# Gate rows of a two-block decoder kernel computed in the norms' gaps instead of inside the feed-forward loops

## What is computed

```
mod = cond @ ada_w[l] + ada_b[l]
sh1, sc1, g1, sh2, sc2, g2, sh3, sc3, g3 = split(mod, 9)
hn = rms_norm(h, norm_g[l, 0]) * (1 + sc1) + sh1
h = h + 0.5 * g1 * swiglu(hn, ffn1_w_in[l], ffn1_w_out[l])
hn = rms_norm(h, norm_g[l, 1]) * (1 + sc2) + sh2
h = h + g2 * (mixed(hn @ w_in[l]) @ w_out[l])
hn = rms_norm(h, norm_g[l, 2]) * (1 + sc3) + sh3
h = h + 0.5 * g3 * swiglu(hn, ffn2_w_in[l], ffn2_w_out[l])
```

## Time and profile before

| | us |
|---|---|
| median of 3 runs | 2203.54 |
| lowest, highest | 2200.04, 2205.11 |
| the profiled execution | 2208.43 |
| its span | 2206.4 |
| PE busy in the span | 2117.9 |
| DVE busy | 1413.1 |
| ACT busy | 1109.4 |
| POOL busy | 60.6 |

### The profile page before, as it was taken

The page is one execution under the profiler, slowest core; times in us unless marked ns, Lnnn a source line. Parts: engine busy times, 40 slices in busy tenths (PEclk is TensorE's granted clock), DMA queues, the critical chain, the costliest instruction groups (busy, mean ns, idle before and its releaser), DMA issues.

```text
span 2206.4 us, 33404 instructions
## 1 busy us (share of the span) xinstructions
PE 2117.9 (96%) x13908; PEld 1910.1 (87%) x13908; DVE 1413.1 (64%) x1866; ACT 1109.4 (50%) x1757; POOL 60.6 (3%) x40
## 2 busy tenths in 40 slices
PE   8999899999999999999999999899999999989999
PEld 7798788998979888999899898589989998868998
DVE  5466568786455748878655665665576556566555
ACT  5347535445426835444555553555555555355554
POOL 0110000000020000000001000000000100000000
PEclk9999999999999999999899998899999999889999
DMA  7353278895544238988455432145545554213553
GB/s 265 115 191 115 77 276 332 345 365 187 172 137 150 96 114 320 367 336 332 168 184 179 155 134 93 63 154 188 182 152 199 173 188 149 81 58 134 181 184 133
DMA packets 56165, 409.54 MB, mean 186 GB/s; under 512 B 6608, under 2 KB 6992, under 8 KB 7888
## 3 DMA queue, kind: packets, MB, share of 16 engines
q1 hardware_dynamic: 46512, 330.20, 42.1%
q10 hardware_dynamic: 9504, 77.21, 8.8%
HBM read 406.34 MB, written 1.05 MB: 185 GB/s over the span
## 4 chain that ended last, share of the span: by engine, by line
PE 85%; DVE 7%; ACT 5%; issue 2%; DMA 1%; POOL 0%; DVEq 0%; ACTq 0%; SPq 0%; POOLq 0%
PE bank L555 24%; PE bank L556 24%; PE bank L557 24%; PE bank L974 3%; PE bank L1049 1%; DVE weights_low L388 1%; PE bank L1699 1%; PE bank L907 1%; ACT weights_high L377 1%; PE bank L919 1%; ACT work L435 1%; ACT scratch L452 1%; DVE work L513 1%; ACT work L436 0%; ACT weights_high L378 0%
## 5 line engine op out<-in xcount | busy, mean ns | idle before, releaser
L388 DVE TENSOR_TENSOR weights_low<-raw_weights,weights_high 128x1024 fp32r<-128x1024 f32 x584 | 699.8, 1239 | 457.2 <-ACT weights_high L377 455.6
L555 PE MATMUL bank<-h_high,weights_high 128*128 128x256 f32 x2944 | 859.3, 292 | 18.7 <-DVE h_low L524 13.1
L556 PE MATMUL bank<-h_low,weights_high 128*128 128x256 f32 x2944 | 846.9, 288 | 0.0
L557 PE MATMUL bank<-h_high,weights_low 128*128 128x256 f32 x2944 | 846.5, 288 | 0.0
L377 ACT ACTIVATE weights_high<-raw_weights 128x1024 fp32r<-128x1024 f32 x292 | 309.0, 1058 | 725.2 <-PE bank L557 681.4
L555 PEld LDWEIGHTS bank<-h_high,weights_high 128*128 128x128 f32 x2944 | 578.9, 197 | 33.9 <-DVE work L513 11.6
L556 PEld LDWEIGHTS bank<-h_low,weights_high 128*128 128x128 f32 x2944 | 579.2, 197 | 3.9 <-issue 1.9
L557 PEld LDWEIGHTS bank<-h_high,weights_low 128*128 128x128 f32 x2944 | 578.5, 197 | 0.0
L378 ACT ACTIVATE weights_high<-raw_weights 128x1024 fp32r<-128x1024 f32 x292 | 305.1, 1045 | 0.0
L555 PE MATMUL bank<-weights_high,hidden_high 128*128 128x512 f32 x608 | 237.9, 391 | 2.4 <-DVE weights_low L388 2.4
L556 PE MATMUL bank<-weights_low,hidden_high 128*128 128x512 f32 x608 | 237.6, 391 | 0.0
(11 more groups left out here) (275 smaller groups left out, 2010.7 us busy)
## 6 DMA issues: line engine op xcount, KB each, us to landing
raw_weights<-in_stream SPq DMA_DIRECT2D x310, 1024.0 KB, 4.9
work<-in_ada ACTq DMA_DIRECT2D x64, 1152.0 KB, 10.1
consts<-in_consts SPq DMA_DIRECT2D x1, 2048.0 KB, 12.5
work<-in_row ACTq DMA_DIRECT2D x2, 836.0 KB, 5.5
x<-in_x SPq DMA_DIRECT2D x1, 1024.0 KB, 4.9
out_x<-x SPq DMA_DIRECT2D x4, 256.0 KB, 2.0
gain_row<-in_final SPq DMA_DIRECT2D x1, 512.0 KB, 13.1
vec<-in_vec SPq DMA_DIRECT2D x1, 169.0 KB, 12.5
```

Source lines behind the costliest of these rows:

```text
L388: dve.tensor_tensor(low[:, c], raw[:, c], high[:, c].bitcast(F32), ALU.subtract).then_inc(m.raw_done[plan.index[name] % RAW], 1)
L555: pe.matmul(out, aH, bH, start=start, stop=False, skip_group_check=True)
L556: pe.matmul(out, aH, bL, start=False, stop=False, skip_group_check=True)
L557: return pe.matmul(out, aL, bH, start=False, stop=stop, skip_group_check=True)
```

## The change

The two products, their wait and ACT's two copies move from the loops of the feed-forward parts into the norm's gap: gate 0 ahead of the transposes of n1, gate 1 ahead of those of n2, gate 2 ahead of those of n3. They now use banks 4 and 5 (6 and 7 for the very first), whose sums DVE has read by then, which is what the wait on x_ready says. The groups row0 to row2 leave GROUPS2, so six groups a layer fewer are handed round on banks 0 to 3. ACT copies behind its last 1/rms and ahead of its first rounding of h. POOL makes the diagonals earlier: gate 0 in the feed-forward part of the stage before (behind up4 of the first block, or behind fg2_4), gate 1 still in feed-forward 1, gate 2 when mc0 has been used. The squares go to `h_temp` in `work`, so that `scratch` can hold diagonals across a norm. Behind the 16 transposes PE makes two products of the identity with itself, 128 columns, whose result is not read (`pe_keep`).

```diff
@@ ffn of pe_layer2
+            if j == 1:
+                pe.wait_ge(m["row_copied"], m.at("row_copied", 2 if n == 1 else 6))
...
-            if j in ROWS_AT[n]:
-                r = ROWS_AT[n][j][0]
-                pe.wait_ge(m["diag_ready"], m.at("diag_ready", r + 1))
-                for half in range(2):
-                    name = f"row{r}_{half}"
-                    pe_begin(pe, m, plan, name)
-                    done(name, pe.matmul(m.bank(plan, name)[:, :], m.const("ones"), diag(m, r)[:, half * 512:half * 512 + 512],
-                                         start=True, stop=True))
@@ new functions
+def row_bank(m, plan, r, half):
+    return m.ps[4 + half if r > 0 or plan.l > 0 else 6 + half]
+def pe_row(pe, m, plan, r, s):
+    pe.wait_ge(m["diag_ready"], 3 * plan.l + r + 1)
+    for half in range(2):
+        if r < 2:
+            pe.wait_ge(m.x_ready, m.at("x_ready", 4 * s + half + (1 if r > 0 or plan.l > 0 else 3)))
+        pe.matmul(row_bank(m, plan, r, half)[:, :], m.const("ones"), diag(m, r)[:, half * 512:half * 512 + 512], start=True,
+                  stop=True).then_inc(m["row_full"], 1)
+def pe_keep(pe, m, bank, n):
+    for _ in range(n):
+        pe.matmul(bank[:, 0:P], m.const("ident"), m.const("ident"), start=True, stop=True)
+def act_row(act, m, plan, r):
+    for half in range(2):
+        act.wait_ge(m["row_full"], m.at("row_full", 2 * r + half + 1))
+        act.activation(gate_row(m, r)[:, half * 512:half * 512 + 512], row_bank(m, plan, r, half)[:, :],
+                       ACT.Copy).then_inc(m["row_copied"], 1)
@@ pe_layer2
+    pe_row(pe, m, plan, 0, -1)
     pe_norm(pe, m, plan, -1, "n1")
+    pe_keep(pe, m, m.ps[6] if l > 0 else m.ps[5], 2)
     ffn(1, 0, "n1")
+    pe_row(pe, m, plan, 1, 0)
     pe_norm(pe, m, plan, 0, "n2")
+    pe_keep(pe, m, m.ps[6], 2)
...
+    pe_row(pe, m, plan, 2, 1)
     pe_norm(pe, m, plan, 1, "n3")
+    pe_keep(pe, m, m.ps[6], 2)
@@ act_layer2
     for i in range(4):
         norm_square(act, m, step, 0, PIECES_DOWN, i)
+    act_row(act, m, plan, 1)
     norm(1, "n2")
@@ norm_square
-    step(act.activation(sq_tiles(m)[:, c], m.x[:, c], ACT.Square, accum_out=stat(m, tt, 0 if first else 1)))
+    step(act.activation(h_temp(m)[:, c], m.x[:, c], ACT.Square, accum_out=stat(m, tt, 0 if first else 1)))
@@ pool_layer2
+        elif name == "mo0":
+            m.wait_consumed(pool, plan, "mc0")
+            diagonal(pool, m, l, 2)
+        elif name == "fg2_4" and plan.next is not None:
             m.wait_full(pool, plan, name)
-            diagonal(2, 32)
+            diagonal(pool, m, l + 1, 0)
```

More of the change, by code:

```diff
@@ L97, in ffn_groups @@
         out += [(f"fg{n}_{j}", "V"), (f"fu{n}_{j}", "V")]
-        if j in ROWS_AT[n]:
-            out += [(f"row{ROWS_AT[n][j][0]}_{h}", "A") for h in range(2)]
     return out
@@ L188 @@
     2: {"a_copied": 8, "conv_diag": 3, "conv_exp": 2, "conv_log": 1, "conv_normed": 2, "conv_rstd": 1, "conv_sq": 1,
[L189 to L194, removed]
+         "conv_step": 34, "down_used": 22, "fgate_exp": 22, "fgate_log": 22, "fox_l": 1, "fox_lf": 1, "gelu_act": 4,
+         "gelu_vec": 6, "gv_ready": 2, "hH_ready": 24, "h_ready": 12, "lam_exp": 1, "lam_sum": 1, "ln_rstd": 1, "ln_stat": 1,
+         "mix_high": 4, "mix_low": 4, "o_ready": 6, "o_sq": 2, "p_ready": 8, "pad_zero": 1, "pv_done": 8, "row_copied": 6,
+         "row_full": 6, "rstd_ready": 6, "scored": 12, "soft_exp": 24, "softplus_done": 26, "sum_ready": 8, "top": 12,
+         "turned": 8, "uH_ready": 22, "uL_ready": 22, "ws_ready": 1, "x_added": 12, "x_ready": 12, "xn_ready": 12,
+         "y_copied": 4, "z_ready": 4, "z_rstd": 5, "z_sq": 4},
 }
@@ L231 @@
 SIGNALS = (
-    "angle_ready", "trig_ready", "cond_exp", "cond_ready", "ada_last",
+    "angle_ready", "trig_ready", "cond_exp", "cond_ready", "ada_last", "row_full", "row_copied", "modx_ready",
     "a_copied", "a_mla", "a_ret", "a_sb", "act_step", "comb_ready", "conv_done", "conv_exp", "conv_normed",
@@ L1510, in modx, with diagonal @@
     return m.modx[:, 40 * l:40 * l + 40]
+def diagonal(pool, m, l, r):
+    pool.wait_ge(m["modx_ready"], l + 1)
+    cols8 = mod(m, l, 40, 8) if r == 1 else modx(m, l)[:, 24 + 4 * r:32 + 4 * r]
+    pool.tensor_tensor(tiles(diag(m, r), 8), wide(m.const("ident"), 8), cols8.unsqueeze(2).to_broadcast([P, 8, P]),
+                       ALU.mult).then_inc(m["diag_ready"], 1)
 def pool_layer1(pool, m, plan):
@@ L1516, in pool_layer1 @@
     for name in plan.groups:
-        if name.startswith("rsw"):
+        if name == "up4" and plan.l == LAYERS - 1:
+            m.wait_full(pool, plan, name)
+            diagonal(pool, m, 0, 0)
+        elif name.startswith("rsw"):
             g = int(name[3:])
@@ L1796, in pe_layer2 @@
     pe_pair(pe, m, plan, "cg")
+    pe.wait_ge(m["row_copied"], m.at("row_copied", 4))
     pe.wait_ge(m["z_ready"], m.at("z_ready", 2))
@@ L1860, in ffn @@
                 at_event(split_high, act, m, plan, f"fd{n}_{j - 1}")
[L1861 to L1866, removed]
     def head_scale(name, k):
@@ L1947, in extras @@
             mix_high(act, m, mixed, MIX_ORDER[n])
+    act_row(act, m, plan, 0)
     norm(0, "n1")
@@ L2005, in act_layer2 @@
         norm_square(act, m, step, 1, PIECES_OUT, i)
+    act_row(act, m, plan, 2)
     norm(2, "n3")
@@ L2063, in ffn @@
         r, s = (0, 0) if n == 1 else (2, 2)
-        m.wait_freed(dve, plan, f"row{r}_1")
+        dve.wait_ge(m["row_copied"], m.at("row_copied", 2 * r + 2))
         for i, (tt, half) in enumerate(PIECES_DOWN):
@@ L2256, in vec_layer2 @@
     at_event(split_low, dve, m, plan, "mc1")
+    dve.wait_ge(m["row_copied"], m.at("row_copied", 4))
     for i, (tt, half) in enumerate(PIECES_OUT):
```

18 lines of the change are left out of this document (3 added, 15 removed).

## The result

| | before | changed |
|---|---|---|
| median, us | 2204.32 | 2185.53 |
| lowest, highest | 2200.04, 2210.17 | 2184.33, 2190.4 |
| runs, taken together | 4 | 4 |
| profiled execution, its span | 2208.43, 2206.4 | 2185.22, 2183.1 |

The ratio is 0.9919, with an interval from 0.9898 to 0.994. The forecast was 2193.6 us with a range from 2187.0 to 2199.5, so the gain was undersized: -18.8 us measured, -9.9 in the sum. The runs for experiment g1 repeated the comparison with more executions of before: 2186.19 us of 4 against 2208.29 of 7, ratio 0.9902 [0.9885, 0.9918].

A forecast was written before the change was run, and what follows sets the result against it. PE, busy for 96% of the span, was taken as the bound. Terms -10.3 + 1.0 - 0.6 gave -9.9 us, so 2193.6 us from a median of 2203.54, with a range from 2187 to 2199.5.

The forecast's parts named there:

- The clock behind a gap ... 0 for the sum: PE's first products after a gap: the clock falls later in the gap, comes back where it did; 0 us.
- Rival 1: The clock holds in the gaps, 1.6 to 2 us gained at n2 and n3 gaps; chance 0.2.
- Its form with n3 alone: The clock holds only in both gaps before n3: -14 us in sum, 2189.6 us.
- Its form with all gaps: The clock holds in all six gaps, with 1 to 2 us gained at each: 2183.8 us.
- Six gates out of the loops: Feed-forward loops on PE: each gate removed saves 1.71 us, 10.3 us in all.
- The gap holds one gate: Gaps before n2, n3 and n1 of layer 1: 1.71 us of products fit into 2.16 us, cost 0.
- rival 2: The gap is too small, transposes come 0.5 to 1 us late in five gaps; 2197.5 us, chance 0.12.
- ACT's copies: Two copies in the gap, 1.2 us, fit into ACT's 2.99 us of idle time; cost 0, gain 0.
- Transposes at the full clock: Two gaps before n3: DVE's wait for the transposes shortens by some 0.3 us each, 0.6 us gained.
- POOL's diagonals: Six diagonals made at other places: cost 0, upper bound 0.6 us each, 3.6 us in all.
- Gap n1 of layer 0: Gate's products at half clock take 3.42 us; the gap grows by 1.0 us, between 0.3 and 1.5.

The follow-up runs named there:

- g1: The changed kernel itself, unchanged, run in more rounds beside the kernel before: 2186.19 us against 2208.29, ratio 0.9902.
- e1: The changed kernel without its idle products behind the transposes: 2191.04 us, ratio 0.9934 against before.
- e2: The kernel before with only the two idle products added behind the transposes of each gap: 2199.77 us, ratio 0.9966.
- e4: The changed kernel with 12 or 8 idle products in each gap instead of two: 2182.36 us, ratio 0.9891 against before.
- f7: The changed kernel with the gate's products made twice in the gaps: 2195.91 us, ratio 0.9946 against before.
- f5: The kernel before, gates still in the loops, plus two unread fp32 products of 512 columns ahead of each gap's transposes: 2203.58 us, ratio 0.9983.
- h3: The changed kernel a third time, unchanged, one run: 2187.73 us.
- f8: e4 with the first block's rows of 36 one-column products issued as three times 12: 2174.13 us, ratio 0.9855 against before.
- f6: The kernel before, gates in the loops, with unread gate-sized products ahead of the transposes and two idle products behind: 2199.96 us, ratio 0.9975.

## Why the prediction was wrong

**The failed step is "The clock behind a gap ... 0 for the sum".** I wrote that the clock would fall later in the gap and come back where it did. It does not fall at all before n3, and before n2 it falls for 3.4 us (once for 6.8) instead of 10.2. I argued from the largest idle piece, 2.87 us, which keeps its length. That is a row of n2, and I took it for all gaps. In the gap before n3 of the kernel before, the last piece is 1.52 us, and the largest is the first, 2.00 us, which the change fills:

```profile
1437.42 1.97 PE L478 MATMUL bank<-consts,work 128*128 128x128 f32 x8 [0.25 <-DVE work L465]
1440.91 0.55 PE L555 MATMUL bank<-h_high,weights_high 128*128 128x256 f32 x1 [1.52 <-DVE h_low L524]
```

Before n2 the largest piece stayed (2.96 us), and the time at the low level still shrank, so it is not the largest piece alone that decides. Before n3 the clock holds with 0.28, 0.28 and 1.70 us, falls with 0.28, 0.28 and 2.15 (e1), and falls earlier with 2.00, 0.16 and 0.67 (e2). Before n2 it holds with 0.28, 0.34 and 0.73 (e4). These are observations and no rule: f7 lost the clock with less idle time than the changed kernel, and equal pieces gave unequal low stretches (f5, h3). It also matters when it falls: in e2 the low level is over by the time the dense stream starts, so it costs nothing in feed-forward 2. What this is worth, by the floors: the four feed-forward stages of before, in their order, stood 0.9, 2.1, 0.7 and 2.1 us over them, those of the changed kernel 0, 0, 0.7 and 0. That is -5.1 us, and 0.6 us more at the start of each mixing stage, -6.3 in all.

**Rival 1 was the case, for n3.** Its 2 us for each of these gaps are the 2.1 measured. Its 1.6 for n2 was too much: the stage behind it gained 0.6, as its second and third pair of h tiles are late either way. Its form with n3 alone, 2189.6 us, is 4 us off. Its form with all gaps, 2183.8, is the nearest of my numbers, 1.7 us off, but by luck: it had 1.6 us for each n2, 1.6 for n1 of layer 0 and 1 for n1 of layer 1, where 0.6, 0.9 and 0 were measured, and nothing for the rest of the mixing stages. I gave it 0.2 because the row of one gap with pieces of 2.00, 0.34 and 2.87 us had lost the clock. But this row had both long pieces, and the change fills one and shortens what is behind the transposes; it was no evidence on that case. The Trainium skill (TensorE: Matmul & The Clock Gate, "Why this matters for your kernels") pointed the right way: no long idle gap between bursts. The changed kernel before n3 and five of the six gaps of e4 agree with it. e1 and e2 show that it isn't enough: before n3 the clock fell with no idle piece over 2.15 us. f8 adds a case without idle time.

**The mixing stages were missing from the sum.** They gave -5.2 us. I named only the first 6 us behind the gap and looked at no other low stretch. Only 1.2 of these 5.2 us are explained; the cause of the other 4 stays open.

**What held.**
- Six gates out of the loops, 10.3 us: 3.42 and 1.70 by the floors. PE was the bound there, and nothing became late.
- The gap holds one gate: its products end 0.28 us ahead of the transposes, whose distance to the last product is the same. Two gates are too much for it (f7), and rival 2's shortage did not occur.
- ACT's copies cost 0. Line 1666 took 585 and 592 ns in the median, two of them from 1261.41 to 1262.48, and the rounding of h waited 2.02 us more for DVE (2.99 in the earlier trace rows).
- Transposes at the full clock: -0.25 us before each n3, forecast -0.3.
- POOL's diagonals cost 0. Behind mc0 a pair of splits took 3.01 us where 2.36 stood alone, near the 2.92 of the earlier trace rows, and no stage shows it. But the bound of 0.6 us a place was too small. Behind up4 of the first block the diagonal (4.05 us long) met an instruction of DVE on 2304 columns, and the pair of splits after that took 4.05 us, 1.7 more than alone, near the 1.9 that the prediction had as the worst of a place. PE has no idle piece there, from 898 to 915 us.

**What was off by a little.** Gap n1 of layer 0 grew by 1.6 us, against 1.0 with a bound of 1.5. The row is this:

```profile
1056.97 5.50 PE L1052 MATMUL bank<-consts,work 128*128 128x1 f32 x36
1062.33 3.76 PE L1653 MATMUL bank<-scratch,consts 128*128 128x512 f32 x4
1065.89 2.06 PE L469 MATMUL bank<-consts,work 128*128 128x128 f32 x16
```

The gate's 3.76 us at the low level are as worked out (3.42 by distance of starts, 3.56 here). The 36 one-column records ahead of it took 5.50 us instead of the 4.45 in the earlier trace rows, as the clock fell on the way; that I had not counted. In e1 and e4, where the low level ended sooner, the gap was 11.49 us, with the gate in it for nothing.

The terms for the whole: -10.3 (forecast -10.3), +1.6 (+1.0), -0.5 (-0.6), clock at the feed-forward stages -5.1 (0), mixing -5.2 (0), first block -1.4 (0, perhaps chance). Their sum is the -20.8 of the mean spans; the timed medians differ by 18.8 and, in g1, by 22.1.

## What to carry to other kernels

Work of PE that waits for nothing in the loop and holds nothing up there (broadcasts by a matrix of ones, for example) belongs in the gaps where PE waits for another engine, up to the length of the first idle piece and no further. Count such a move twice: once for the stream that it leaves, and once for the clock that the filled gap may keep, in the dense stream behind it; price the latter at the distance between the stage's length and its length at the full clock. Before that, list all stretches at the low level in the whole kernel, since those behind very short products cost as much as those behind gaps, and need no idle time to arise.

## What the runs showed that I had not expected

- Two idle products in a gap, 0.43 us together and read by nobody, are worth 5 to 7 us over six gaps (e2 -7.5; the changed kernel against e1 -4.9).
- PE loses the clock without being idle: behind 36 fp32 records of one column, with PE busy for 14.00 of 14.00 us, the granted clock was 0.76; in three groups of 12 it was 1.00. In three profiles each of before and of f6, the 4-column products of the mixing stage were followed by 17.1 us at the low level, in both layers, every time; in f5, in layer 0, by 6.8 us.
- When the clock falls matters too. Behind the gaps before n3, a fall just ahead of the dense stream was followed by 6.8 us at the low level (e1), and one that came before the transposes' end (e2) by 3.4, over as the stream began.
- Identical code differs by up to 4 us in a stage of 160 us (158.58 to 162.83) and by 3.4 us over the first block, from these stretches alone. A gain of 4 us in a kernel like this one is read from stages in several profiles, not from one span.
